# Second stack of a 4-layer network in one kernel: attention by head pairs, half tiles of the pooled output product between its steps, pooled values on GpSimd, logits by head pairs

## The reference

```python
h = rms_norm_2(x, g_pre_mix[l])
u_pool, q, k, v, iq, ik, iw = jnp.split(h @ w_in[l], SPLIT_POINTS, axis=-1)
# q, k, iq, ik get a partial rotary embedding; 8 heads of 64; iw is scaled by 8 ** -0.5
a_out = pool_mixer(u_pool, w_pool[l], pool_scale[l])    # windows 2, 4, 8, 16 for the 4 groups of 128 channels
b_out = dsa_attention(q, k, v, iq, ik, iw, topk)        # topk = 128
mix = jnp.concatenate([a_out, b_out], axis=-1) @ w_out[l]
x = x + rms_norm_2(mix, g_post_mix[l])
f = jnp.square(jax.nn.relu(rms_norm_2(x, g_pre_ffn[l]) @ w_ff1[l])) @ w_ff2[l]
x = x + rms_norm_2(f, g_post_ffn[l])
# pool_mixer, group g of window w:  d = (sum of the last w tokens) / min(t + 1, w) - u;  y = (d @ w_pool[g]) * pool_scale
# dsa_attention: score = sum over 8 heads of iw * relu(iq . ik * 64 ** -0.5), keys of later 64-token chunks excluded
#   per query the 128 keys of highest score are kept; softmax attention over them, 8 heads of 64
```

## Time and profile before

| | before |
|---|---|
| median of 3 runs | 2718.42 (2717.82 to 2722.79) |
| the profiled execution, whole | 2726.11 |
| its span | 2724.3 |
| busy: TensorE, weight loads | 2514.8 (92%), 1979.5 (73%) |
| busy: VectorE, ScalarE, GpSimd | 1541.6 (57%), 841.4 (31%), 318.6 (12%) |
| mean granted TensorE clock | 0.954 of full |

### The profile page before, as it was taken

One profiled execution on the slowest core, in us unless ns is written; L12 is line 12 of the kernel. 1 busy time (PEld: TensorE's weight loads), 2 busy tenths in 40 slices (PEclk: granted clock), 3 DMA queues, 4 the chain that ended last, 5 costly groups with the idle time before them and its releaser, 6 DMA issues. The chain is left out here.

```text
span 2724.3 us, 29127 instructions
## 1 busy us (share of the span) xinstructions
PE 2514.8 (92%) x11206; PEld 1979.5 (73%) x11206; DVE 1541.6 (57%) x2228; ACT 841.4 (31%) x1211; POOL 318.6 (12%) x191
## 2 busy tenths in 40 slices
PE   7988999998988999999788998999968889899996
PEld 5866888886776788888656566888855656688885
DVE  6774544455775544455569737444456974644444
ACT  4454222233435322223321433222232133322222
POOL 1011000011010100001116112000031420200002
PEclk9999999998999999999789898999978989899998
DMA  3211222222220223222111111232221110123222
GB/s 142 101 63 47 94 107 93 93 93 92 78 86 32 92 93 108 92 93 93 43 58 65 44 47 62 93 108 92 92 71 62 62 47 32 54 101 106 94 92 77
DMA packets 33300, 217.74 MB, mean 80 GB/s; under 512 B 4128, under 2 KB 4384, under 8 KB 7840
## 3 DMA queue, kind: packets, MB, share of 16 engines
q1 hardware_dynamic: 33184, 216.18, 22.3%
HBM read 214.07 MB, written 2.10 MB: 79 GB/s over the span
## 5 line engine op out<-in xcount | busy, mean ns | idle before, releaser
L323 PE MATMUL ps<-gh,wh 128*128 128x512 f32 (+1 forms) x1728 | 702.8, 407 | 87.0 <-DVE gl L464 66.1
L323 PE MATMUL ps<-gl,wh 128*128 128x512 f32 (+1 forms) x1728 | 685.2, 397 | 0.0
L323 PE MATMUL ps<-gh,wl 128*128 128x512 f32 (+1 forms) x1728 | 683.6, 396 | 0.0
L307 ACT ACTIVATE wh<-wr 128x2048 fp32r<-128x2048 f32 x196 | 374.0, 1908 | 588.0 <-PE ps L323 588.0
L313 DVE TENSOR_TENSOR wl<-wr,wh 128x2048 fp32r<-128x2048 f32 x174 | 398.6, 2291 | 254.2 <-ACT wh L307 254.2
L323 PE MATMUL ps<-hh,wh 128*128 128x512 f32 x1280 | 501.4, 392 | 7.4 <-DVE hl L944 3.1
L323 PE MATMUL ps<-hh,wl 128*128 128x512 f32 x1280 | 499.0, 390 | 0.0
L323 PE MATMUL ps<-hl,wh 128*128 128x512 f32 x1280 | 498.8, 390 | 0.0
L323 PEld LDWEIGHTS ps<-gh,wh 128*128 128x128 f32 (+1 forms) x1728 | 330.1, 191 | 188.2 <-DVE gl L464 73.9
L323 PEld LDWEIGHTS ps<-gl,wh 128*128 128x128 f32 (+1 forms) x1728 | 330.5, 191 | 74.2 <-issue 6.0
L323 PEld LDWEIGHTS ps<-gh,wl 128*128 128x128 f32 (+1 forms) x1728 | 330.2, 191 | 73.0
(11 more groups left out here) (202 smaller groups left out, 2521.4 us busy)
## 6 DMA issues: line engine op xcount, KB each, us to landing
wr<-in_weights SPq DMA_DIRECT2D x198, 1024.0 KB, 4.7
x<-in_xt SPq DMA_DIRECT2D x1, 2048.0 KB, 11.8
out_yt<-x SPq DMA_DIRECT2D x1, 2048.0 KB, 7.2
tmp<-in_positions SPq DMA_DIRECT2D x4, 256.0 KB, 3.2
arena<-in_gates SPq DMA_DIRECT2D x2, 512.0 KB, 3.8
arena<-in_embed SPq DMA_DIRECT2D x2, 512.0 KB, 5.6
par<-in_params_b SPq DMA_DIRECT2D x2, 274.0 KB, 3.2
par<-in_params_a SPq DMA_DIRECT2D x2, 157.5 KB, 2.6
```

The lines of the kernel that those rows point to most:

```text
L307: act.activation(mem.wh[:, c % 2, :], mem.wr[:, c % 2, :], ACT.Copy).then_inc(sem["high"], 1)
L323: done = pe.matmul(out, stationary, moving, start=(first and n == 0), stop=(last and n == 2), skip_group_check=True)
```

## The change

1. **Logits by head pairs.** 12 entries of (query block, pair of heads). The two matmuls of a pair go to two banks (6, 7 and 4, 5 in turn), with one Relu over both. A pair goes ahead of every second inner step of three tiles (both of chunk 4, the first of chunk 5).
2. **Pooled values on GpSimd.** The three VectorE instructions of `pool_values` are gone; GpSimd scales the window sum in place, multiplies its first 16 columns by the counts and subtracts u.
3. **Attention by head pairs.** 16 steps, two heads each: scores in banks 1, 2 and 3, 4 in turn; one maximum over both; two exponents; two scalings; transposes in banks 5 and 6; one copy back; weighing after each step, by 128 columns, the two heads into the two halves of the partitions of bank 7. Scores are two steps ahead instead of three.
4. **Output product in two parts.** The output matrix comes in half chunks, the rows of the pooled values first (`B_POOL`, two chunks, eight tiles of 4 inner steps), then those of attention (`B_ATT`, two chunks, eight tiles of 4). After the transposes of each step TensorE does half a pooled tile in bank 0 (6 matmuls); VectorE copies a finished tile to `branch`. The attention part comes after and is added to `branch`. In its first chunk the inner step is the outer loop, over four tiles. GpSimd makes three low halves (chunks 11, 12, 13) instead of two. `branch` lies elsewhere in the arena, so it is zeroed in two parts.

```diff
-B_OUT = 11
-B_FF = B_OUT + BC
+B_POOL = 11
+B_ATT = B_POOL + 2
+B_FF = B_ATT + 2
...
-    STEPS = QT * HEADS2
+    STEPS = QT * HEADS2 // 2
...
-    LOGITS = [(i, h) for i in range(1, QT) for h in range(HEADS2)]
+    LOGITS = [(i, j) for i in range(1, QT) for j in range(HEADS2 // 2)]
...
@block.gpsimd
-                    last.then_inc(sem["windowed"], 1)
+                    own.settle()
+                    own.mark(pool.tensor_scalar(source[:, W - S + PAD:W], source[:, W - S + PAD:W], 1.0 / WINDOWS[g], None, ALU.mult))
+                    own.mark(pool.tensor_tensor(source[:, PAD:2 * PAD], source[:, PAD:2 * PAD], cst[:, C_CNT + PAD * g:C_CNT + PAD * (g + 1)],
+                                                ALU.mult))
+                    own.settle()
+                    if g:
+                        pool.wait_ge(sem["pool_product"], g)
+                    pool.tensor_tensor(pooled, source[:, PAD:W], u[:, g, PAD:W], ALU.subtract).then_inc(sem["pooled_ready"], 1)
...
-                split_low(pool, mem, sem, B_OUT)
-                split_low(pool, mem, sem, B_OUT + 1)
+                for c in range(B_POOL, B_ATT + 1):
+                    split_low(pool, mem, sem, c)
...
@block.scalar
-                    act.activation(tmp[:, s % 2, 0:n], ps[:, 6 + s % 2, 0:n], ACT.Relu, scale=DH ** -0.5).then_inc(sem["rectified"], 1)
-                    if s == 1:
+                    act.activation(tmp[:, 2 * b:2 * b + 2, 0:n], ps[:, LOGIT_BANKS[b]:LOGIT_BANKS[b] + 2, 0:n], ACT.Relu,
+                                   scale=DH ** -0.5).then_inc(sem["rectified"], 1)
+                    if s == 3:
                         split_high(act, mem, sem, 5, b_used(5))
...
                 for s in range(STEPS):
                     if s + 1 < STEPS:
                         exponents(s + 1)
+                    if s > QT and s % QT == 1:
+                        pair_high(s // QT - 1)
                     untangle(s)
-                    if s >= 8 and s % 8 == 2:
-                        pair_high(s // 8 - 1)
-                    if s == 4:
-                        split_high(act, mem, sem, B_OUT + 1, b_used(B_OUT + 1))
+                    if s == 0:
+                        split_high(act, mem, sem, B_POOL + 1, b_used(B_POOL + 1))
+                    if s == STEPS // 2:
+                        split_high(act, mem, sem, B_ATT, b_used(B_ATT))
                 pair_high(3)
-                for c in range(B_OUT, B_FF):
...
+                for c in (B_ATT, B_ATT + 1):
+                    split_high(act, mem, sem, c + 1, b_used(c + 1))
+                    for t in range(4):
+                        k = 4 * (c - B_ATT) + t
                         act.wait_ge(sem["drained"], B_TILE[c] + t + 1)
-                        square_slice(act, mem, sem, 1, 2 * (c - B_OUT) + t, branch)
+                        square_slice(act, mem, sem, 1, k, branch(k))
...
@block.vector
-                        if t == 0:
-                            pool_values(c - B_Q)
-                        elif c > B_Q:
+                        if t and c > B_Q:
                             pool_low(c - B_Q - 1)
                         picks(1)
...
                 for s in range(STEPS):
                     scale_rows(s)
+                    if s and s % 2 == 0:
+                        keep_pooled(s // 2 - 1)
+                    if s > QT and s % QT == 1:
+                        pair_low(s // QT - 1)
                     if s + 2 < STEPS:
                         maxima(s + 2)
-                    if s >= 8 and s % 8 == 3:
-                        pair_low(s // 8 - 1)
+                keep_pooled(KT - 1)
                 pair_low(3)
-                dve.wait_ge(sem["low"], split_count(B_OUT + 1))
...
+                dve.wait_ge(sem["low"], split_count(B_ATT))
+                for c in (B_ATT, B_ATT + 1):
+                    split_low(dve, mem, sem, c + 1)
+                    for t in range(4):
+                        tile, k = B_TILE[c] + t, 4 * (c - B_ATT) + t
                         dve.wait_ge(sem["product"], tile + 1)
-                        dve.tensor_copy(branch[:, 2 * (c - B_OUT) + t, :], ps[:, tile % 4, :]).then_inc(sem["drained"], 1)
+                        dve.wait_ge(sem["drained"], B_TILE[B_ATT])
+                        dve.tensor_tensor(branch(k), branch(k), ps[:, tile % 4, :], ALU.add).then_inc(sem["drained"], 1)
...
@block.tensor
-                product_tile(pe, mem, sem, 4, 0, B_TILE[4], mem.gh, mem.gl, before=three_logits)
-                product_tile(pe, mem, sem, 4, P, B_TILE[4] + 1, mem.gh, mem.gl)
-                linear_chunk(5, mem.gh, mem.gl)
+                product_tile(pe, mem, sem, 4, 0, B_TILE[4], mem.gh, mem.gl, before=logits_before(0))
+                product_tile(pe, mem, sem, 4, P, B_TILE[4] + 1, mem.gh, mem.gl, before=logits_before(4))
+                product_tile(pe, mem, sem, 5, 0, B_TILE[5], mem.gh, mem.gl, before=logits_before(8))
+                product_tile(pe, mem, sem, 5, P, B_TILE[5] + 1, mem.gh, mem.gl)
...
+                def weigh(s):
+                    j, i = divmod(s, QT)
+                    pe.wait_ge(sem["untangled"], s + 1)
+                    if i == 0 and j:
+                        pe.wait_ge(sem["pair_low"], j)
                     for k in range(i + 1):
+                        for e in range(2):
+                            last = pe.matmul(ps[DH * e:DH * (e + 1), 7, P * i:P * (i + 1)], v[:, k, DH * (2 * j + e):DH * (2 * j + e + 1)],
+                                             pt[:, s % 2, e, k, :], start=(k == 0), stop=(k == i), skip_group_check=True)
                     last.then_inc(sem["weighted"], 1)
...
+                def pooled_part(s):
+                    n, part = divmod(s, 2)
+                    c = B_POOL + n // 4
+                    if s % 8 == 0:
+                        pe.wait_ge(sem["low"], split_count(c))
+                    if part == 0:
+                        pe.wait_ge(sem["drained"], B_TILE[B_POOL] + n)
+                    half_tile(c, n % 4, 0, (2 * part, 2 * part + 1), 0, part == 1)
...
+                scores(0)
+                scores(1)
                 for s in range(STEPS):
-                    if s + 3 < STEPS:
-                        scores(s + 3)
+                    if s + 2 < STEPS:
+                        scores(s + 2)
                     turn(s)
-                    if s >= QT and s % QT == 1:
-                        weigh(s // QT - 1)
-                weigh(HEADS2 - 1)
+                    pooled_part(s)
+                    if s:
+                        weigh(s - 1)
+                weigh(STEPS - 1)
...
-                for c in range(B_OUT, B_FF):
-                    linear_chunk(c, mem.hh, mem.hl, mixer_ready if c == B_OUT else None)
+                for k in range(4):
+                    pe.wait_ge(sem["pair_low"], k + 1)
+                    for t in range(4):
+                        half_tile(B_ATT, t, (B_TILE[B_ATT] + t) % 4, (k,), 4, k == 3)
+                pe.wait_ge(sem["low"], split_count(B_ATT + 1))
+                for t in range(4):
+                    tile = B_TILE[B_ATT + 1] + t
+                    pe.wait_ge(sem["drained"], tile - 3)
+                    half_tile(B_ATT + 1, t, tile % 4, range(4), 4, True)
```

More of the change, by code:

```diff
@@ L1327, in _ @@
                 pool.wait_ge(sem["updated"], KT)
-                pool.memset(branch[:, :, :], 0.0).then_inc(sem["zeroed"], 1)
+                for at, tiles in zip(B2_BRANCH, (6, 2)):
+                    pool.memset(ar[:, at:at + tiles * S], 0.0).then_inc(sem["zeroed"], 1)
                 gather_squares(pool, mem, sem, 3)
@@ new lines, in scores @@
+                    n, b = P * (i + 1), s % 2
+                    if s >= 2:
+                        pe.wait_ge(sem["exped"], 2 * (s - 1))
+                    for e in range(2):
+                        half = slice(DH * e, DH * (e + 1))
+                        pe.matmul(ps[:, 1 + 2 * b + e, 0:n], qk[half, j, P * i:n], qk[half, 4 + j, 0:n],
+                                  start=True, stop=False, skip_group_check=True)
+                    for e in range(2):
+                        last = pe.matmul(ps[:, 1 + 2 * b + e, 0:n], mem.idb[:, :], mask[i], start=False, stop=True,
+                                         skip_group_check=True)
@@ L1765, in weigh @@
-                def weigh(h):
-                    j = h // 2
-                    pe.wait_ge(sem["untangled"], QT * (h + 1))
-                    if h % 2 == 0 and j >= 2:
-                        pe.wait_ge(sem["pair_low"], j - 1)
-                    out = ps[DH * (h % 2):DH * (h % 2 + 1), 6 + j % 2, :]
-                    for k in range(QT):
-                        last = pe.matmul(out[:, P * k:S], v[:, k, DH * h:DH * (h + 1)], pt[h % 2][:, k, P * k:S],
-                                         start=(k == 0), stop=(k == QT - 1), skip_group_check=True)
-                    last.then_inc(sem["weighted"], 1)
@@ new lines, in half_tile @@
```

(9 more changed lines are left out.)

213 lines of the change are left out of this document (99 added, 114 removed).

## The result

The changed kernel takes 2647.18 us (median of four runs, 2645.80 to 2649.76); the kernel before, timed beside it, 2719.62 (2717.82 to 2722.79). The ratio is 0.9734, with an interval of 0.9717 to 0.9750: 72.4 us faster. The forecast was 2663 with a range of 2632 to 2690. The sign and the range hold; the gain is 17 us larger than the 55 of the sum. The profiled executions, 2726.11 and 2649.76, stand 6.5 and 2.6 over these medians, so what follows, read from them, shows some 4 us more of gain than the medians do.

A forecast was written before the change was run, and what follows sets the result against it. The prediction took TensorE to bound logits, attention and product, and VectorE the picks. Savings of 3.7 + 11.1 + 12.2 = 27 us a layer, 55 with both layers and 1 for idle times, gave 2663, range 2632 to 2690.

The forecast's parts named there:

- Logits, 3.7 forecast: Second stack's logits by head pairs: last weighing 32.9 us after the first logit instead of 36.6, saving 3.7 a layer.
- The 8.3 us of holding: In the logits, GpSimd holds VectorE for a low half, a window sum and three new operations, 8.3 us.
- 29.2 for the three tiles: In the logits, twelve pairs at 1.07 at most (12.8 us) and 72 product matmuls at 0.228 (16.4) take 29.2.
- Pooled values, 11.1 forecast: Among the picks, moving pooled values to GpSimd frees 25.1 us of VectorE, less 14 of holds: 11.1 a layer.
- now VectorE goes on to its picks and meets GpSimd in the multiply: Among the picks, multiply L1554 is held: 2.4 us four times and 1.5 three times, together 14.
- Attention and product, 12.2 forecast: Attention and output product take 100.2 us a layer (74.5 + 25.7) instead of 112.4, saving 12.2.
- Around it: ... 13: Attention, beyond four pairs' TensorE work: first step's chain, half clock, held scalings and small waits cost 13 us.
- Laying the product between the steps of a full TensorE gains nothing by itself: In attention, only fewer TensorE cycles, the low clock and VectorE's 96.8 us can gain, not placing product matmuls between steps.
- (1): Attention's weighing: column halves go one after another, 9.2 us more a layer on TensorE; 2663 becomes 2673; chance 0.25.
- (2): Among the picks, VectorE and GpSimd hardly meet; saves 12 us a layer more, 2639; chance 0.17.
- (3): Attention steps are bound by the chain of maximum, exponent, scaling and turn, 5.5 us each: 88 for attention, 2690; chance 0.08.
- (4): GpSimd becomes the bound of the second stretch; at 12 us more a group the kernel takes 2736; chance 0.02.

## Why the prediction was right, and where its sizes were off

**What bounds it, and the three terms' signs: right.** VectorE sets the picks (80.1 busy of 81.6), TensorE the logits and attention. Each part costs time when it alone is undone: single logits 3.6 us a layer, pooled values 13.5, the scores' neighbourhood 13.0, the laid-in product 14.4. Of the signs that the prediction named, the last weighing came at 30.3 for 33, the stretch from there to the first scores at 87.3 for 85, and the scores of a pair in the time of one.

**Logits, 3.7 forecast, 1.8 came.** The pieces: last weighing 33 us after the first logit forecast, 30.3 measured. I had 1.5 of stall and 1 of clock; there were none: VectorE was held in both L1507 (4.00; 0.42 without a neighbour, in the kernel with single logits) and in some of the seven weighings behind it, and TensorE, pairs ahead, never waited for it. The 8.3 us of holding were taken too high: over their sizes these eight instructions lost 5.3. Part of it is a wrong reading of the earlier trace rows: the two weighings of the kernel before, 5.77 together, are 4.56 and 1.10 when read one by one, the first ending 0.28 behind the low half (1393.23 against 1392.95), so VectorE was let in between. And luck is in the 29.2 for the three tiles, where 29.1 was measured: a pair costs 0.63, 0.84 or 1.06 by its columns and not 1.07 always (10.1 for 12.8), but the six product matmuls between two pairs take 1.58, not 1.37 (19.0 for 16.4). What I left out was the work behind the last weighing: the sum ended there, and the edges (L1516), 0.7 us when free, met the low half of the next chunk and took 5.09. Moving them ahead of it gave back 4.8. The price of the three new operations on GpSimd was low too: the scaling takes 1.45 to 1.77, where I took 1.0, and the three together 3.0 to 3.7 against 2.6.

**Pooled values, 11.1 forecast, 14.1 came.** The step "now VectorE goes on to its picks and meets GpSimd in the multiply" was right, with 12.7 of holds, 11.8 of them new, for 14. Its two halves were off in opposite directions: the second multiply of a pair is held by 1.4, 2.9, 3.2 and 4.2 (11.6, forecast 9.6), growing as the window sums grow and GpSimd runs later; the first by 1.1 in all, where I had 4.5. Undoing the part costs 13.5, between the bounds of 4 and 23. The Trainium skill, "GPSIMD Engine Reference", section "Key points", has the rule that GpSimd shares its SBUF interfaces with VectorE and contends with VectorE's instructions with two SBUF inputs. This case's traces agree where GpSimd's operation has two inputs (a multiply of 0.68 at 4.90 under a low half, which is waited out to its end), and don't where it has one: under GpSimd's scaling such a multiply took 0.68 and 0.89. So of the three new operations only the subtraction weighs much in VectorE's way.

**Attention and product, 12.2 forecast, 23.3 came: the term that was mis-sized.** The TensorE work was right: 15.4 a pair of heads forecast, 15.2 measured. The tail was about right: from the last product matmul to the first of the next stage, 13.9 after against 11.5 before, 2.4 more where I had 3.4. The error is "Around it: ... 13", the waits and the clock. I took the first step's wait of 3.45 from the first stack, 3 of half clock, 2 of holds and 4.5 of small waits; together they are 4.6 (5.4, if a pair's work is taken as 15.0). Two reasons, both read against the kernel with the product after the steps. There the waits and the clock do cost 17.8, so they exist, and even the 13 was no exaggeration for steps without cover; but half a tile of product, six matmuls of 0.23, stands in each step between the turn and the weighing, and that is time in which the next chain runs. And the clock comes up early and stays up. These are windows of the changed kernel's first steps:

```profile
1505.00:1507.20 2.20, 2.20 (x7) 0.90 (x8) 1.29 (x5) 1.02 (x4) 0.00 (x0) 0.52 0.01 4
1507.20:1510.00 2.80, 2.79 (x13) 1.51 (x13) 1.81 (x5) 2.41 (x3) 0.15 (x1) 1.00 0.00 0
```

Full clock (2.4 GHz) from 1507.2 on, 4.5 us into attention, where before the first 21.4 had 0.60. In the kernel with the product after the steps it was at 1.00 from 1506 to 1508 too, but back at 0.50 from 1512 to 1515, behind the wait of 3.62. Why it comes up sooner than in the kernel before, the runs don't separate.

So the sentence "Laying the product between the steps of a full TensorE gains nothing by itself" doesn't hold for the changed kernel: pairs cut TensorE's work for four steps to 9.7 us without the product, while four steps of the chain take 14.2 (56.7 for sixteen), and the product fills what the pairs open. Whether it was true of the kernel before isn't shown, since no run lays the product into single heads. Of the 23.3 in the third column 9.0 came without laying in and 14.3 with it.

**The rivals.** (1) Column halves one after another: wrong. Sixteen weighing parts take 1.03 to the next start in the changed kernel and 1.89 when put in one half, worth 7.3 a layer; the forecast of 2.6 a pair of heads stands at 2.8 (0.37 + 0.59 + 0.81 + 1.03). The Trainium skill, "TensorEngine Tiling (Array Packing)", section "Key Properties", says that different tiles run independently; no row of before showed it for columns, and these runs do. (2) VectorE and GpSimd hardly meet: no, 12.7 us a layer, though the time came out nearer to this rival's 2639 than to the forecast. It came out there by another term, which is why the stage table and not the total must decide. (3) Steps bound by the chain: it is what happens when the product isn't laid in, and then with 56.7 for attention alone. (4) GpSimd the bound: no; TensorE waits for it 8.4, 2.0 and 3.5 us in the picks, but VectorE, though held, is idle only 1.5 us in all, and the stage is VectorE's.

**What was left on the table.** The order of GpSimd's work and of three small additions is worth 7 us a layer more: 2633.5 or 2632.0 instead of 2647.2, 0.966 and 0.965 of the kernel before. The two can't be told apart; both lie clearly under the change's 0.9734.

## What to carry to other kernels

When work moves to GpSimd, list what VectorE will run during each long GpSimd operation, up to and past the end of your stage: here its two-input and scalar operations on SBUF waited out a low half whole, and MAX8, MATCH_REPLACE8 and operations that read PSUM didn't, so such GpSimd operations belong under the latter. Ask also what GpSimd runs: its two-input operations held VectorE, its scaling next to nothing. Two matmuls on opposite row halves cost as one if they are neighbours, so keep the pairs adjacent and put the masks behind both. A stage whose TensorE work has become shorter than its chain is the place for a dense product: cost the waits with the filler in place, not from the stage without it.

## What the runs showed of the hardware

- Two chains of matmuls on opposite column halves overlap even when they come as two groups and not in turn: sixteen parts 1.09 in turn, 1.58 in two groups, 1.96 on one half. Opposite row halves with one bf16 matmul between them don't overlap at all: 1.05 for each two parts, where four took 1.06.
- GpSimd's scaling (one input) doesn't hold VectorE's two-input operations on SBUF as its two-input operations do: a multiply of 512 columns begun inside a scaling takes 0.68 to 0.89, inside a low half up to 5.02, where it takes 0.68 alone.
- VectorE gets in between two GpSimd operations that follow at once: in the kernel before, a weighing of 0.48 took 4.56 under a low half and ended 0.28 behind it, and the next took 1.10 under the window sum.
- On GpSimd a scaling in place of 496 columns (one input) takes 1.45 to 1.77, more than a window sum of 527 columns with two inputs (1.19; four of up to 527 columns in a row 4.71).
- Making a low half costs VectorE 2.28 to 2.68; letting GpSimd make it (4.5 to 4.7) costs VectorE up to 4.3 in a single held multiply.
